# Two 1024-wide input projections (gating values, queries) as seven block products instead of eight, with the modulation sums moved around them

## What is computed

```python
mod_l = jnp.split(silu_c @ w_mod[l] + b_mod[l], 6, axis=-1)     # 2048 x 12288
hl = modulate(rms_norm(xl, norm1_g[l]), mod_l[0], mod_l[1])
zl = hl @ w_in[l] + b_in[l]                                     # a1, a2 | su, sv | q | k | v | 3 gates
# convolution over 31 taps of a1 * sigmoid(a2); gelu(su) * spatial(layer_norm(gelu(sv)))
# attention of q over neighbours k, v and the context's k, v
xl = xl + mod_l[2] * (gated sum of the three branches @ w_o + b_o)
hl2 = modulate(rms_norm(xl, norm2_g[l]), mod_l[3], mod_l[4])
xl = xl + mod_l[5] * ffn(hl2)
```

## Time and profile before

| | us |
|---|---|
| median of 3 runs | 3057.09 |
| lowest and highest of the 3 | 3053.69, 10490.25 |
| profiled execution, device time | 3051.51 |
| its span, first to last instruction | 3049.7 |
| PE busy in the span | 3003.1 (98%) |
| DVE busy | 2095.9 (69%) |
| ACT, POOL busy | 333.0, 71.6 |

### The profile page before, as it was taken

How to read it: one execution, slowest core, us unless ns; L and a number is a source line. 1 busy time by engine, 2 the same in 40 slices (tenths; PEclk the granted TensorE clock), 3 DMA queues, 4 the chain that set the end, 5 groups by cost and what they waited for, 6 DMA issues and landing times.

```text
span 3049.7 us, 51983 instructions
## 1 busy us (share of the span) xinstructions
PE 3003.1 (98%) x22771; PEld 2777.3 (91%) x22783; DVE 2095.9 (69%) x3176; ACT 333.0 (11%) x659; POOL 71.6 (2%) x137
## 2 busy tenths in 40 slices
PE   6999999999999999999999999999999999999998
PEld 3688847999999999999999999999999998899998
DVE  1039976368866677766778877867667576995765
ACT  1021010032220000111010000001012102000010
POOL 0000001010000000000000000000000000000000
PEclk9999999999999999999999999999999999999999
DMA  8999975354445555755777555565444654544443
GB/s 297 318 315 291 285 258 197 115 166 139 128 150 166 194 166 169 188 166 166 249 249 249 166 166 166 166 180 177 142 139 139 209 179 124 152 139 111 125 152 111
DMA packets 586543, 561.54 MB, mean 184 GB/s; under 512 B 24573, under 2 KB 556624, under 8 KB 578893
## 3 DMA queue, kind: packets, MB, share of 16 engines
q1 hardware_dynamic: 554464, 466.65, 49.9%
q0 software_dynamic: 13856, 80.90, 7.4%
q10 hardware_dynamic: 17997, 10.67, 1.3%
HBM read 549.66 MB, written 8.51 MB: 183 GB/s over the span
## 4 chain that ended last, share of the span: by engine, by line
PE 86%; DVE 9%; DMA 4%; issue 1%; ACT 0%; SPq 0%; DVEq 0%; ACTq 0%; POOLq 0%
PE psum L495 39%; PE psum L475 15%; DVE arena L2026 3%; PE psum L668 3%; PE psum L571 2%; DVE arena L1960 2%; DMA arena<-w_mod 2%; PE psum L564 2%; PE psum L545 2%; PE psum L606 2%; PE psum L917 2%; PE psum L932 2%; PE psum L922 2%; PE psum L925 2%; PE psum L931 2%; PE psum L930 2%
## 5 line engine op out<-in xcount | busy, mean ns | idle before, releaser
L475 PE MATMUL psum<-arena,ring 128*128 128x256 f32 (+2 forms) x3200 | 756.1, 397 | 0.6 <-ACTq L1222 0.6
L475 PEld LDWEIGHTS psum<-arena,ring 128*128 128x128 f32 x3200 | 604.2, 190 | 138.5 <-issue 63.5
L495 PE MATMUL psum<-arena 128*128 128x128 f32 x6144 | 702.8, 275 | 0.3 <-DVE arena L1827 0.3
L495 PEld LDWEIGHTS psum<-arena 128*128 128x128 f32 x6144 | 694.4, 192 | 7.2 <-issue 6.2
L495 PE MATMUL psum<-arena,ring 128*128 128x128 f32 x4224 | 486.1, 275 | 0.0
L495 PEld LDWEIGHTS psum<-arena,ring 128*128 128x128 f32 x4224 | 479.0, 192 | 0.3
L1813 DVE TENSOR_TENSOR arena<-ring 128x2048 f32<-128x2048 f32 x100 | 229.2, 2292 | 277.6 <-PE psum L495 249.6
L1792 DVE TENSOR_TENSOR arena<-ring,arena 128x1024 f32<-128x1024 f32 (+1 forms) x188 | 183.2, 974 | 5.9
L1792 DVE TENSOR_TENSOR arena<-arena 128x512 f32<-128x512 f32 (+7 forms) x268 | 142.4, 531 | 16.3 <-DVE arena L2774 5.7
L1960 DVE SCALAR_TENSOR_TENSOR arena<-arena,cvec 128x2048 f32<-128x2048 f32 x45 | 105.7, 2348 | 42.2 <-DMA arena<-w_mod 41.8
L2623 DVE TENSOR_TENSOR arena<-ring 128x1024 f32<-128x1024 f32 x64 | 78.4, 1225 | 69.4 <-PE psum L917 68.6
(11 more groups left out here) (357 smaller groups left out, 3293.4 us busy)
## 6 DMA issues: line engine op xcount, KB each, us to landing
ring<-w_ff SPq DMA_DIRECT2D x128, 1024.0 KB, 6.5
ring<-w_in SPq DMA_DIRECT2D x88, 1024.0 KB, 7.6
ring<-ab_w_in SPq DMA_DIRECT2D x56, 1024.0 KB, 5.6
arena<-w_mod POOLq DMA_DIRECT2D x48, 1024.0 KB, 7.0
ring<-cd_w_in SPq DMA_DIRECT2D x48, 1024.0 KB, 5.8
ring<-w_mod SPq DMA_DIRECT2D x32, 1024.0 KB, 6.4
ring<-w_in SPq DMA_DIRECT2D x32, 512.0 KB, 4.5
ring<-w_o SPq DMA_DIRECT2D x16, 1024.0 KB, 6.0
```

The lines of the kernel that those rows point to most:

```text
L475: mm = pe.matmul(psum[:, s, m * N:(m + 1) * N], w[:, k, m * P:(m + 1) * P], x(k)[:, 0:N], start=(j == 0), stop=(j == kt - 1))
L495: return pe.matmul(o, z, w, **kw) if tokens else pe.matmul(o, w, z, **kw)
```

## The change

1. sv and q are taken out of the plain way and done by `pair`: four pairs each, one after the other on PE, with the weight preparations, the combining and the hand-over to ACT placed between tap groups 13 to 20. In the stream their slots are now 2048 x 256 in two.
2. The taps come first. No chunk is added before the taps are done. DVE waits for all taps of a group before going on.
3. Of the 48 chunks 32 remain in this part: 16 during k, 16 inside v's pairs (3, 3, 3, 3, 2 and 2 after the halves of pairs 1 to 3). The third set (feed-forward scale) is loaded by a new loop of POOL after the attention and added in gate_sgu and gate_att (`add_gate_chunk`, one per pair for pairs 5 to 8, two for pairs 9 to 14), summed before out_att's third slot.
4. X is written out right after su instead of during k. The sums for the layer norms and the spatial product move back by one tile of k. The bias tables are loaded one gate pair later and masked in gate pairs 2, 4, 5 and 6 instead of 1 to 4.

```diff
-    ("su", "w_in", SU, 2, 16, 128), ("sv", "w_in", SV, 2, 16, 128),
-    ("q", "w_in", WQ, 2, 16, 128), ("k", "w_in", WK, 2, 16, 128), ("v", "w_in", WV, 2, 2, 256),
+    ("su", "w_in", SU, 2, 16, 128), ("sv", "w_in", SV, 2, 2, 256),
+    ("q", "w_in", WQ, 2, 2, 256), ("k", "w_in", WK, 2, 16, 128), ("v", "w_in", WV, 2, 2, 256),
...
+CHUNK_AT = (20, 22, 24, 26, 28, 28, 28, 29, 29, 29, 30, 30, 30, 31, 31, 31,
+            34, 35, 36, 36, 37, 37, 38, 38, 38, 39, 39, 39, 40, 40, 40, 40)
...
@@ PE @@
-            beside("sv", HL, "act", alone, ahead=ahead_of_sv)
-            beside("q", HL, "act", alone)
+            pe.wait_ge(sem("input_sums"), n["input_sums"].next())
+            for p in range(4):
+                pair(p, halves(HL, SQ0), TX)
+            for p in range(4):
+                pair(p, halves(HL, SQ0), TX)
             pe.wait_ge(sem("ctx_normed"), n["ctx_normed"].next())
-            beside("k", H, "act", beside_k, N=2 * T, ahead=ahead_of_k)
+            beside("k", H, "act", beside_k, N=2 * T)
...
@@ ACT @@
-            beside("sv", tiles("sv", ZV, ACT.Gelu_apprx_tanh, (cols, COL["b_in"] + SV // P)), alone)
+            load(kept[0], at(0, 4096), "load_x_out")
             settled("uv_ready")
...
+            for p in range(4):
+                act.wait_ge(sem("pair_ready"), n["pair_ready"].next())
+                for m in range(2):
+                    i = 4 * (p % 2) + 2 * m
+                    ins = A(ZV[:, 2 * p + m, :].rearrange("p (a t) -> p a t", a=2), STAGEA[:, i:i + 2, :],
+                            ACT.Gelu_apprx_tanh, bias=col("b_in", SV // P + 2 * p + m))
+                ins.then_inc(sem("stage_taken"), n["stage_taken"].up())
...
@@ POOL @@
-            for j in range(48):
+            for j in range(32):
...
+            pool.wait_ge(sem("att_ready"), 1)
+            for k in range(KT):
+                pool.wait_ge(sem(f"chunk{k % 2}_used"), n[f"chunk{k % 2}_used"].next())
+                pool.dma_start(GCHUNK[k % 2], w[:, k, 4096 + 2 * D:4096 + 3 * D]).then_inc(sem(f"load_chunk{k % 2}"), 16)
...
@@ DVE @@
             for g in range(24):
                 for m in range(11 * g, min(11 * g + 11, TAPS * HT)):
                     tap(m)
-                if g == 12:
-                    mod_columns(0, 7)
-                if g in CHUNK_PARTS:
-                    add_chunk(chunk)
-                    chunk += 1
+                v.wait_ge(sem("vector_step"), n["vector_step"].now())
+                if g == 11:
+                    quarter_sums(HL, SQ0, "input_sums")
+                    v.wait_ge(sem("load_x_out"), 16)
+                    w = pair_differences("sv", 0, TX)
+                    pair_sums(0, w, TX)
+                elif 13 <= g < 21:
+                    i = g - 13
+                    p = i % 4
...
+                    elif i < 7:
+                        w = pair_differences(("sv", "q")[i // 4], p + 1, TX)
+                        pair_sums(p + 1, w, TX)
+                    if i >= 2:
+                        v.wait_ge(sem("stage_taken"), i - 1)
+                    pairs_added(p, STAGEA)
+                    v.sem_inc(sem("pair_ready"), n["pair_ready"].up())
...
-            chunk = chunks(3)
+            chunk = chunks(4)
             centre()
-            chunk = chunks(3)
+            chunk = chunks(2)
             layer_norm_scale(ZV, "sgu_ln_g", "sgu_ln_b")
             v.sem_inc(sem("ln_out"), n["ln_out"].up())
+            chunk = chunks(2)
             layer_norm_sums(CV, CSQ, 6)()
-            mod_columns(1, 7)
-            chunk = chunks(6)
+            chunk = chunks(8)
...
-            chunk = chunks(6)
-            v.wait_ge(sem("load_x_out"), 16)
             w = pair_differences("v", 0, TX)
             pair_sums(0, w, TX)
-            chunk = chunks(4)
             for p in range(4):
                 for h in range(2):
...
                     v.sem_inc(sem("pair_ready"), n["pair_ready"].up())
+                    if p > 0:
+                        chunk = chunks(3 if p < 3 else 2)
...
                 if p == 4:
                     quarter_sums(ATT, SO, "out_sums")
+                elif 5 <= p < 9:
+                    add_gate_chunk(p - 5)
+                elif 9 <= p < 15:
+                    add_gate_chunk(2 * p - 14)
+                    add_gate_chunk(2 * p - 13)
```

More of the change, by code:

```diff
@@ L1965, in add_chunk, with add_gate_chunk @@
                     v.sem_inc(sem("mod_added"), n["mod_added"].up())
+            def add_gate_chunk(k):
+                v.wait_ge(sem(f"load_chunk{k % 2}"), n[f"load_chunk{k % 2}"].next())
+                if k == 0:
+                    ins = v.tensor_scalar(GACC, GCHUNK[k % 2], cond[:, k:k + 1], None, ALU.mult)
+                else:
+                    ins = v.scalar_tensor_tensor(out=GACC, in0=GCHUNK[k % 2], scalar=cond[:, k:k + 1], in1=GACC,
+                                                 op0=ALU.mult, op1=ALU.add)
+                ins.then_inc(sem(f"chunk{k % 2}_used"), n[f"chunk{k % 2}_used"].up())
+                v.wait_ge(sem(f"chunk{k % 2}_used"), n[f"chunk{k % 2}_used"].now())
+                if k == KT - 1:
+                    v.sem_inc(sem("mod_added"), n["mod_added"].up())
             def add_late(k):
@@ L2013, in _ @@
                 v.wait_ge(sem(free("dve", s)), n[free("dve", s)].now())
-                for j in range(2 * s, 4 * s + 2):
-                    add_chunk(j)
             def tap(m):
@@ L2224, in first_taken @@
             def first_taken(p):
-                v.wait_ge(sem("stage_taken"), 8 + p - 1)
+                if p == 1:
+                    mod_columns(1, 7)
+                    v.sem_inc(sem("mod_done"), n["mod_done"].up())
+                    step(v.tensor_copy(cond[:, :], cvec[:, :, 0]))
+                    done()
+                v.wait_ge(sem("stage_taken"), 16 + p - 1)
                 if p == 7:
@@ L2296, in _ @@
                 into_mixed(STAGEA[:, 4 * e:4 * e + 4, :], 2 * q, "mixed")
+                if q == 2:
+                    mod_columns(2, 7, at(18432, KT, 32))
+                    step(v.scalar_tensor_tensor(out=gain[:, 2, :], in0=mod[:, 64:64 + KT, 0], scalar=1.0,
+                                                in1=col("norm2_g", 0, KT), op0=ALU.add, op1=ALU.mult))
+                    done()
             v.sem_inc(sem("gate_used"), n["gate_used"].up())
```

78 lines of the change are left out of this document (40 added, 38 removed).

## The result

The changed kernel takes 3083.2 us (median of 4 runs, 3082.11 to 3083.51) against 3055.0 before (the middle of 3 runs, 3053.69 to 3057.09; a fourth, stray one took 10490.25 and is left out): 28 us more, ratio 1.0092 with a 95% interval of 1.008 to 1.0104. By 2% that is no change, as forecast, but the time lies 0.2 us above the range, and the size was forecast at 11 us. The profiled execution took 3083.2 us, its span is 3081.4.

The account below looks back on a forecast made before the run. PE, busy 98% of the span, was taken to bound the kernel. Terms -10.4 + 9.3 + 7.6 - 3.2 + 7.2 + 0.4 = +10.9 us gave 3062.4, stated as 3064 on the measured scale; range 3047 to 3083.

Parts of the forecast that it names:

- The rest: Third chunk set in the gates, bias loads and moved modulation sums: zero, at most 5 us if ring and chunks hinder.
- The clock: Half clock after long PE waits: 0 to 1.7 us a fall for the X and k waits, 0.4 us counted.
- The gain: Sv and q: eight pairs of seven products instead of 16 tiles save PE 10.4 us.
- Wait 1, X written out: Start of sv: PE waits 7.9 us for weights prepared on X's place after its write; 9.3 with the second pair.
- The 1.3 in the second pair: Sv's second pair: PE waits 1.3 us more for weights queued behind DVE's first wait.
- The other pairs: Sv and q from the third pair on: DVE needs 11.2 us against PE's 12.5 a pair, so no wait.
- The rival of the half clock in every pair: Sv and q paced by DVE, PE at half clock between pairs: 3154 us, chance 0.03.
- Wait 2, the spatial product in k: K: a burst of eight chunks, 31.3 us, delays DVE's first spatial bank; PE waits 7.6 us.
- The rival of quick reloads: Chunk reloads in k and v take 5.0 us instead of 6.5: 3053 us, chance 0.27.
- Wait 3, chunks in v: V: bursts of three chunks put DVE behind; PE waits 5.4 us in pair 3, 1.8 at first gate pair: 7.2.
- the old waits that went: Earlier PE waits of 3.0 us in v's first pair and 0.2 in k disappear: 3.2 us saved.
- The slow reloads: Rival: chunk reloads take 8.0 us, both queues wanting 335 GB/s in v's bursts: 3079 us, chance 0.20.

Follow-up runs that it names:

- all3: Changed kernel with bias loads in four groups, X's load early, VectorE's chunks reordered in k and v, and modulation sum behind v's first pair: 3042.17 us, ratio 0.9963.
- dose7: Kernel before the change, with the first sum of k's spatial product repeated seven more times ahead of it by VectorE: 3055.98 us, single run.
- bias: Changed kernel with POOL's 32 bias loads spread again in four groups of eight, nothing else: 3070.76 us.
- doses: Kernel before the change, with four, seven or eleven repeated VectorE sums ahead of k's spatial product: 3060.5, 3055.98 and 3062.66 us, single runs.
- all2: Changed kernel with the four single edits together, and TensorE's modulation sum moved between the halves of v's first pair: 3047.41 us, ratio 0.9982.
- all: Changed kernel with four edits together: bias loads grouped, X's load early, k's chunks split five and three, v's chunks two per half: 3048.61 us, ratio 0.9984.
- ksplit: Changed kernel with three of the eight chunks ahead of k's second spatial product moved behind v's input sums, nothing else: 3076.97 us.
- vspread: Changed kernel with v's sixteen chunks as two behind each half, and the modulation's sum and columns moved ahead: 3070.91 us.

## Why the prediction was wrong

Two steps failed. "The rest" put the bias loads at zero, and they cost 8.24 us of wait and 2.1 of clock. "The clock" put the half clock at 0.4 us for three waits, and it cost 9.2 behind them.

Against `all3`, which has none of the four waits, the changed kernel loses 663.01 - 621.16 = 41.85 us, and the table splits it: su to k 11.45 (8.40 wait, 3.05 clock), k to v 10.90 (8.09 and 2.81), v to the first turn 17.38 (5.85 and 8.24, 3.29 clock), behind it 2.12 of clock. Waits 30.6, clock 11.3. With the 14.0 us gained that is +27.8. "Clock" is here what a wait costs beyond itself. About 0.3 us of each is starting again and not the clock: in before the first half of v's first pair takes 15.73 us (489.79 to 505.52) with its wait of 2.96, and 12.50 in dose7 (497.11 to 509.61) without one, though the clock stood at 1.00.

```profile
505.52 3.74 PE L535 MATMUL psum<-ring,arena 128*128 128x128 f32 x32
```

- **The gain** of 10.4: right. Sv and q took 111.6 us and take 100.2 in `all3`; of the difference 1.1 is the sum that moved.
- **"Wait 1, X written out"**: cause right; 7.9 said, 8.40 measured. The 1.3 in the second pair didn't show, and yet it was rightly worked out: DVE had the second pair's weights at 288.89 + 1.23 = 290.12, PE came for them at 291.89. At full clock PE would have come 3.0 us sooner, at 288.9, and waited 1.2 to 1.3 us. Half clock and wait overlap there, so X's fall made the kernel only about 1.8 us longer than the waits alone would have. (7.9 and 1.3 are 9.2, the 9.3 is a rounding. The "first four groups' worth and eleven more" of taps are the front part's twelve groups; 53 us is twelve times 4.44.)
- **"The other pairs"**: right, no wait from the second pair on. The rival of the half clock in every pair didn't happen.
- **"Wait 2, the spatial product in k"**: right, 7.6 said, 8.1 measured. The burst of eight chunks was worked out at 31.3 us from the mean reload of 6.5; it took 31.5 (439.40 to 470.86). The rival of quick reloads falls for this stage. With it falls here the Trainium skill's price for such a DMA (DMA: Bandwidth & Descriptors, Anatomy of one DMA), from which the prediction worked out its estimate of 5.0 us.
- **"Wait 3, chunks in v"**: near, 7.2 said (5.4 in pair 3, counted from 0, and 1.8 at the first gate pair), 5.85 measured, all in that pair. The nearness is in part luck. It was worked out with 6.5 us for every reload; in v most of those that DVE waited for took 5.6 to 5.9, and two took 10.0 and 8.9, the chunks at 562.58 and 583.18, the second just ahead of the wait. In these two the DMA engines were full (share 1.05 and 1.08 from 550 to 560 us, 1.07 and 1.02 from 575 to 585).
- **"The rest"**: wrong. "The bias loads have a whole pair before the first masking: zero" looked at when the biases are needed and not at what their loads do to others. With `mod_done` later, the groups' waits were for slots already gone by, 32 loads went out back to back, and a ring tile came late: 8.24 us and 2.1 of clock. `bias` shows it.
- **"The clock"**: wrong in size. It counted 0.4 us, with 1.7 as the most for one fall, two falls at most, and one of them mostly paid by the second pair's 1.3 us. The offset of 1.3 was right, as said above. The rest was not: there were four falls, of 3.05, 2.8, 3.3 and 2.1 us. The step took its price from the earlier trace rows, 16 matmuls in the opening, of which only part ran at half clock (5.33 us is less than twice 3.62), and it gave the wait in v no fall at all. The Trainium skill's rule that was weighed there (TensorE: Matmul & The Clock Gate, Part 1) says that an idle array falls to half clock and must be busy again to leave it. The traces agree with it for every wait from 3.5 us on, and show no fall for the wait of 2.96. I should have let it into the sum for every forecast wait.

By place, each with its fall: X 11.45 us for 9.7 counted (+1.8), k 10.9 for 7.6 (+3.3), v 9.1 for 7.2 (+1.9), the gates 10.4 for nothing, and the old waits that went gave 0.4 more than the 3.2 counted. 1.8 + 3.3 + 1.9 + 10.4 - 0.4 = 17.0, which but for rounding is the difference of 27.8 and 10.9. So the unseen wait in the gates with its fall is 10.4 of it, and the three forecast places are 7.0: clock 8.8 more than counted, waits 1.8 less. Either miss alone would have left the time inside the range, at about 3075 or 3072 by the forecast's own scale; `bias`, which is without the first, measured 3071. The slow reloads, the rival nearest to the result, gave 3079 for a reason that held for two reloads in v, and not on the whole.

The range failed with the two steps: it had no room for a wait that wasn't seen, its bound for a fall came from one place in thin work, and it allowed for two falls where three waits were in the sum. That the change came out as no change by 2% was forecast at 0.96 and rests on the small size of the whole, not on these terms.

## What to carry to other kernels

A wait on the engine that bounds the kernel can cost more than itself: here the half clock behind it added 1.4 to 3.3 us to any wait from 3.5 to 9 us, and nothing to one of 3.0. So a plan with several waits loses more than the sum of its waits says, and taking one away is worth more, unless the next wait would have covered the loss, as in sv's second pair. A burst of small loads on one queue is not a matter of its own due time alone: look at what the other queue's tiles do meanwhile, and whether the waits that spaced the loads still hold once they are issued later. Where an engine works in program order, idle time right behind a late step says that the work in front of that step stands on its wrong side.

## What the runs showed of the hardware

- **The fall by its wait.** From the same differences of stages: 3.46 us of wait 1.7, 5.29 2.1, 8.38 2.5 (doses); 3.77 1.9 (`all2`) and 4.28 1.7 (`all`); in k for 7.9 to 8.3 us of wait 2.1 to 3.1; for X, at 8.4 to 9.0 us of wait, 3.0, 2.7, 1.6 and 1.5 in after, `bias`, `ksplit` and `vspread`, whose code is the same there. So it varies by 1.5 us for nearly the same wait. The wait of 2.96 us had none: its stretches 490 to 510 us stood at 1.00.
- **A wait can be paid by the next.** dose7 delays PE by 7.2 us at v's start, and its stretch, 640.66 us, is only 4.3 longer: the wait of 2.96 us in v's first pair is gone, since DVE had the time.
- **The opening isn't constant.** Su starts between 198.93 and 207.89 us in the twelve traces (the three doses at 205.82, 199.09 and 202.61), with PE's work ahead of it the same in all. Before and the doses load a few modulation chunks there and the changed forms none, but both kinds scatter: the four before start at 201.6 on the mean, the eight changed ones at 203.5. The stretch behind varies only where waits do. The clock has a part in it. The five openings that end by 201.80 have a mean clock of 0.99 or 1.00 and 168.1 to 168.9 us of busy PE; the seven that end later have 0.97 or 0.98 and 170.4 to 175.3. PE's idle time in the opening varies too (29 to 35 us), at DMA shares of 0.84 to 0.89. What sets off the longer waits and the falls stays open. It is as large as what a single wait costs, so a single time can't judge such an edit and a trace's stages can.
